# Reading both halves of a product in one VectorE operation: a one-core encoder layer of Strassen-like products

## What is computed

```python
xn = rms_norm(x, attn_norm)
z = xn @ w_in                                   # q | k | v | lru_x | lru_gate | merge gates
attn_branch = windowed_attention(q, k, v) @ w_attn_out
lru_branch  = (rg_lru(conv(xl)) * gelu(yg)) @ w_lru_out
g_a, g_b = split(sigmoid(gl), 2)
x = x + (g_a * attn_branch + g_b * lru_branch) @ w_o
gate, up = split(rms_norm(x, ffn_norm) @ w_gate_up, 2)
x = x + (silu(gate) * up) @ w_down
```

## Time and profile before

| | us |
|---|---|
| median of 3 runs | 1644.11 |
| the profiled execution | 1644.76 |
| its span, first to last instruction | 1643.0 |
| TensorE matmul busy | 1607.5 (98%) |
| VectorE busy | 1027.6 (63%) |
| ScalarE busy | 644.0 (39%) |
| GpSimd busy | 997.6 (61%) |
| granted TensorE clock, mean | 0.993 of full |

### The profile page before, as it was taken

The page is one execution under the profiler, slowest core; times in us unless marked ns, Lnnn a source line. Parts: engine busy times, 40 slices in busy tenths (PEclk is TensorE's granted clock), DMA queues, the critical chain, the costliest instruction groups (busy, mean ns, idle before and its releaser), DMA issues. The chain is left out here.

```text
span 1643.0 us, 28698 instructions
## 1 busy us (share of the span) xinstructions
PE 1607.5 (98%) x11338; PEld 1540.7 (94%) x11338; DVE 1027.6 (63%) x1717; ACT 644.0 (39%) x1322; POOL 997.6 (61%) x714
## 2 busy tenths in 40 slices
PE   7999999999999999999999999999999999999998
PEld 4999999989999898899899989999999999998998
DVE  7677556865646556768798895333333335868695
ACT  5535552354444535424334443333333334333231
POOL 4645543434425251497868529777777778786876
PEclk9999999999999999999999999999999999999999
DMA  5111123213122131373443312222242222373634
GB/s 193 39 52 65 64 72 99 80 66 114 66 97 66 53 114 49 130 291 123 165 149 132 131 39 103 80 78 79 79 184 79 79 79 79 139 271 130 233 142 152
DMA packets 73033, 182.10 MB, mean 111 GB/s; under 512 B 15092, under 2 KB 26676, under 8 KB 72260
## 3 DMA queue, kind: packets, MB, share of 16 engines
q1 hardware_dynamic: 52228, 160.35, 27.7%
q10 hardware_dynamic: 20672, 19.93, 3.8%
HBM read 131.23 MB, written 49.28 MB: 110 GB/s over the span
## 5 line engine op out<-in xcount | busy, mean ns | idle before, releaser
L642 PE MATMUL bank<-xh,wsh 128*128 128x264 f32 x2170 | 620.1, 286 | 8.4 <-DVE spare L1862 3.8
L642 PE MATMUL bank<-xh,wsl 128*128 128x264 f32 x2170 | 616.8, 284 | 0.0
L642 PE MATMUL bank<-xl,wsh 128*128 128x264 f32 x2170 | 616.0, 284 | 0.0
L642 PEld LDWEIGHTS bank<-xh,wsh 128*128 128x128 f32 x2170 | 408.3, 188 | 11.3 <-issue 8.0
L642 PEld LDWEIGHTS bank<-xl,wsh 128*128 128x128 f32 x2170 | 408.4, 188 | 0.2
L642 PEld LDWEIGHTS bank<-xh,wsl 128*128 128x128 f32 x2170 | 408.4, 188 | 0.0
L642 PE MATMUL bank<-acth,wh 128*128 128x352 f32 x960 | 319.3, 333 | 5.6 <-POOL wl L546 4.1
L642 PE MATMUL bank<-acth,wl 128*128 128x352 f32 x960 | 314.7, 328 | 0.0
L642 PE MATMUL bank<-actl,wh 128*128 128x352 f32 x960 | 314.3, 327 | 0.0
L618 POOL TENSOR_TENSOR wsl<-praw,wsh 128x512 fp32r<-128x512 f32 (+1 forms) x157 | 247.6, 1577 | 70.6 <-ACT wsh L1284 70.4
L544 POOL TENSOR_SCALAR wh<-wraw 128x512 fp32r<-128x512 f32 (+1 forms) x100 | 70.9, 709 | 311.9 <-PE bank L642 292.9
(11 more groups left out here) (187 smaller groups left out, 2428.1 us busy)
## 6 DMA issues: line engine op xcount, KB each, us to landing
praw<-in_weights SPq DMA_DIRECT2D x34, 1024.0 KB, 5.0
wraw<-in_weights SPq DMA_DIRECT2D x52, 512.0 KB, 3.3
h_scratch<-ev SPq DMA_DIRECT2D x44, 264.0 KB, 2.1
acc<-h_scratch SPq DMA_DIRECT2D x4, 2112.0 KB, 12.6
ev<-x_scratch SPq DMA_DIRECT2D x6, 1056.0 KB, 5.0
spare<-x_scratch SPq DMA_DIRECT2D x6, 1056.0 KB, 4.9
praw<-in_weights SPq DMA_DIRECT2D x8, 768.0 KB, 5.3
ta_scratch<-tg ACTq DMA_DIRECT2D x24, 176.0 KB, 1.9
```

The costliest lines, as they stand in the source:

```text
L642: return nc.tensor.matmul(*args, **kw)
```

## The change

PSUM is declared as four pairs of banks, so that one access pattern (128 partitions x 2 x 264) covers both halves of a product. In `first_sums` and after products 3 to 6 VectorE does one operation of 528 columns in place of two of 264; it waits for the end of both halves and then counts its semaphore up by 2, so TensorE finds both banks free at once. ScalarE's operations keep their two halves.

Three smaller edits go with it. copy_back is called behind the weights rounded after product 1 instead of those rounded after product 0. In the head, TensorE's `sumsq(1)` goes behind the third raw block; ScalarE gets a small Sqrt between the squares of block 0 and 1, and its rounding of block 0 is cut in two around `root(1)`; VectorE adds block 1's squares in three steps around `rstd(0)`, and `chunk_sum(2)` moves ahead of the second half of `norm(0)` and `rstd(1)`. `combine_hidden` changes as `combine_gated` does and is left out of the diff.

```diff
@@ -390,7 +390,8 @@
             t2raw = tensor(raw, "t2raw", [P, KQ, HALF])
         xl.append(tensor(ctx, "xl6", [P, KQ, HALF], f32r))
 
-        bank = [ctx.enter_context(nc.psum_tensor(f"bank{i}", [P, 512], f32)) for i in range(8)]
+        banks = [ctx.enter_context(nc.psum_tensor(f"banks{i}", [P, 2, 512], f32)) for i in range(4)]
+        bank = [banks[i // 2][:, i % 2, :] for i in range(8)]
@@ -700,8 +701,8 @@
                     raw_block(0, 0)
                     sumsq(0)
                     raw_block(0, 1)
+                    raw_block(0, 2)
                     sumsq(1)
-                    raw_block(0, 2)
                     raw_block(1, 0)
                     sumsq(2)
                     raw_block(1, 1)
@@ -1007,12 +1008,14 @@
                 f(wg[:, 0, c * P:(c + 1) * P], wraw[:, 0, c * P:(c + 1) * P], ACT.Identity, scale=vt[:, c, V_G1:V_G1 + 1])\
                     .then_inc(wg01_done[0], 1)
             squares(0)
+            f(qstd[:, 0, 0:KC], ones[:, 0:KC], ACT.Sqrt)
             squares(1)
             root(0)
             squares(2)
             rstd_row(0)
+            high(0, range(0, 4))
             root(1)
-            high(0, range(KC))
+            high(0, range(4, KC))
             rstd_row(1)
             high(1, range(0, 4))
             root(2)
@@ -1399,7 +1402,7 @@
                             w_high(*made)
                     for made in x_after.get((p, r), ()):
                         x_high(*made)
-                    if r == 0 and p - 1 in (X_FIRST[ATTN_OUT], X_FIRST[OUT]):
+                    if r == 1 and p - 1 in (X_FIRST[ATTN_OUT], X_FIRST[OUT]):
                         copy_back(p - 1)
                     if p == PLAIN - 1 and r == 3:
                         scale_weights()
@@ -1483,12 +1486,18 @@
             for c in range(KC):
                 V.tensor_scalar(wg[:, 1, c * P:(c + 1) * P], wraw[:, 1, c * P:(c + 1) * P], vt[:, c, V_G1:V_G1 + 1], None, ALU.mult)\
                     .then_inc(wg01_done[1], 1)
-            chunk_sum(1, 0, KC, 2)
+            q = xsq[:, 1, :, :]
+            dve.wait_ge(xsq_done, 3)
+            vec(V.tensor_tensor(q[:, 0:2, :], q[:, 0:2, :], q[:, 2:4, :], ALU.add))
             rstd(0)
+            dve.wait_ge(xsq_done, 4)
+            vec(V.tensor_tensor(q[:, 4:6, :], q[:, 4:6, :], q[:, 6:8, :], ALU.add))
+            vec(V.tensor_tensor(q[:, 0:2, :], q[:, 0:2, :], q[:, 4:6, :], ALU.add))
+            V.tensor_tensor(xsum[:, 2, :], q[:, 0, :], q[:, 1, :], ALU.add).then_inc(xchunk_done, 1)
             norm(0, range(0, 4))
+            chunk_sum(2, 0, KC, 3)
+            norm(0, range(4, KC))
             rstd(1)
-            norm(0, range(4, KC))
-            chunk_sum(2, 0, KC, 3)
             norm(1, range(0, 4))
             rstd(2)
             norm(1, range(4, KC))
@@ -1780,18 +1789,24 @@
                 low_done(t, LOWS[t][-1])
                 dve.wait_ge(mm_done, ended(X_FIRST[t], PRODUCTS - 1))
+            def both(r):
+
+                return banks[BANKS[r][0] // 2][:, :, 0:QB]
+
+            def split(a):
+                return a.rearrange("p (n t) -> p n t", t=QB)
+
             def first_sums(p, scale, nres):
 
                 par = (p - PLAIN) % 2 if phase_of(p) == GATE_UP else 0
-                for n in range(2):
-                    q = 2 * nth(p) + n
-                    dve.wait_ge(mm_done, ended(p, 2, n))
-                    dve.wait_ge(s1_done, q + 1)
-                    stt(u2(par, n), bank[BANKS[2][n]][:, 0:QB], scale, u2(par, n), ALU.mult, ALU.add).then_inc(u2_done, 1)
-                    dve.wait_ge(u2_done, q + 1)
-                    if nres:
-                        dve.wait_ge(v_done, 3 * nres)
-                    stt(u4(par, n), bank[BANKS[1][n]][:, 0:QB], scale, u2(par, n), ALU.mult, ALU.add).then_inc(u4_done, 1)
+                q = 2 * nth(p) + 2
+                dve.wait_ge(mm_done, ended(p, 2))
+                dve.wait_ge(s1_done, q)
+                stt(u2(par), both(2), scale, u2(par), ALU.mult, ALU.add).then_inc(u2_done, 2)
+                dve.wait_ge(u2_done, q)
+                if nres:
+                    dve.wait_ge(v_done, 3 * nres)
+                stt(u4(par), both(1), scale, u2(par), ALU.mult, ALU.add).then_inc(u4_done, 2)
@@ -1808,18 +1823,16 @@
                 a = res[b][:, m, :]
                 if r == 4:
                     row_in(p, b)
-                for n in range(2):
-                    dve.wait_ge(mm_done, ended(p, r, n))
-                    if r == 3:
-                        dve.wait_ge(u4_done, 2 * nth(p) + n + 1)
-                    ps = bank[BANKS[r][n]][:, 0:QB]
-                    if r == 4:
-                        stt(a[:, piece(h, n)], a[:, piece(h, n)], 1.0, ps, ALU.add, ALU.mult).then_inc(done, 1)
-                    else:
-                        dst, u = ((u4(0, n), u4(0, n)), None, (u4(0, n), u2(0, n)), (u2(0, n), u2(0, n)))[r - 3]
-                        if r == 5:
-                            dve.wait_ge((merged, gated_done)[t], 3 * p + 1 if t == LRU_OUT else 3 * (p - PAIRS[0]) + 1)
-                        V.tensor_tensor(dst, ps, u, ALU.add).then_inc(done, 1)
+                dve.wait_ge(mm_done, ended(p, r))
+                if r == 3:
+                    dve.wait_ge(u4_done, 2 * nth(p) + 2)
+                if r == 4:
+                    stt(split(a[:, toks(h)]), split(a[:, toks(h)]), 1.0, both(r), ALU.add, ALU.mult).then_inc(done, 2)
+                else:
+                    dst, u = ((u4(0), u4(0)), None, (u4(0), u2(0)), (u2(0), u2(0)))[r - 3]
+                    if r == 5:
+                        dve.wait_ge((merged, gated_done)[t], 3 * p + 1 if t == LRU_OUT else 3 * (p - PAIRS[0]) + 1)
+                    V.tensor_tensor(dst, both(r), u, ALU.add).then_inc(done, 2)
                 dve.wait_ge(done, 2 * nth(p) + 2)
                 half = a[:, toks(h)]
                 if r != 4:
@@ -1851,15 +1864,14 @@
                     return
                 m, h = ((1, 1), (0, 0), (0, 1), (1, 0))[r - 3]
                 done = (c22_done, c11_done, c12_done, c21_done)[r - 3]
-                for n in range(2):
-                    dve.wait_ge(mm_done, ended(p, r, n))
-                    if r != 4:
-                        dve.wait_ge(v_done, 3 * i + {3: 1, 5: 2, 6: 3}[r])
-                    a = res[b][:, m, piece(h, n)]
-                    if p == X_FIRST[OUT] + 1 and r == 3:
-                        x_unused(t)
-                    dst = acc[:, 2 * i + m, piece(h, n)] if t == OUT and p != X_FIRST[OUT] else a
-                    stt(dst, bank[BANKS[r][n]][:, 0:QB], scale, a, ALU.mult, ALU.add).then_inc(done, 1)
+                dve.wait_ge(mm_done, ended(p, r))
+                if r != 4:
+                    dve.wait_ge(v_done, 3 * i + {3: 1, 5: 2, 6: 3}[r])
+                a = res[b][:, m, toks(h)]
+                if p == X_FIRST[OUT] + 1 and r == 3:
+                    x_unused(t)
+                dst = acc[:, 2 * i + m, toks(h)] if t == OUT and p != X_FIRST[OUT] else a
+                stt(split(dst), both(r), scale, split(a), ALU.mult, ALU.add).then_inc(done, 2)
...
```

More of the change, by code:

```diff
@@ L1876, in combine_hidden @@
                 if r != 4:
-                    for n in range(2):
-                        dve.wait_ge(mm_done, ended(p, r, n))
-                        if r == 3:
-                            dve.wait_ge(u4_done, 2 * nth(p) + n + 1)
-                        if r == 5:
-                            dve.wait_ge(h1_done, fp)
-                        dst = (u4(par, n), None, gate(1, n), u2(par, n))[r - 3]
-                        V.tensor_tensor(dst, bank[BANKS[r][n]][:, 0:QB], (u4(par, n), None, u2(par, n), u2(par, n))[r - 3],
-                                        ALU.add).then_inc(done, 1)
+                    dve.wait_ge(mm_done, ended(p, r))
+                    if r == 3:
+                        dve.wait_ge(u4_done, 2 * nth(p) + 2)
+                    if r == 5:
+                        dve.wait_ge(h1_done, fp)
+                    dst = (u4(par), None, gate(1), u2(par))[r - 3]
+                    V.tensor_tensor(dst, both(r), (u4(par), None, u2(par), u2(par))[r - 3], ALU.add).then_inc(done, 2)
                 if r == 6:
```

## The result

The changed kernel takes 1657.13 us (median of 9 runs, 1648.49 to 1662.38) against 1644.11 of the kernel before (9 runs beside it, 1640.82 to 1645.88): a ratio of 1.0072, 95% interval 1.0059 to 1.0086. The forecast was 1648.3, with a range from 1643.4 to 1651.0, so the sign was right and the time was not.

A forecast was written before the change was run, and what follows sets the result against it. TensorE, busy 1607.5 of 1643.0 us, was taken as the bound, so only its gaps counted. Terms of +5.0 (merged reads), 0 (copy_back) and -0.8 (head) gave +4.2 on the 1644.11 median: 1648.3, range 1643.4 to 1651.0.

The forecast's parts named there:

- What bounds the kernel; price of a merged operation: TensorE's gaps bound the kernel; a merged VectorE operation of 528 columns lasts 0.70 us, bounds 0.60 to 0.86.
- The additions 0.55 later and a turn lost: Down projection: VectorE's additions start 0.55 us later, lose a lock turn to GpSimd; waits grow 1.6, 1.6 and 1.25.
- Pair 37, +0.3: Down projection, wait at 1485.28: VectorE was already late, the bank's release comes 0.27 later, so +0.3 us.
- Gate phase and copy_back, 0: The 2.14 us wait at 798.70 goes, but TensorE waits 2.1 longer at 805.15: 0, bounds -1.2 to +0.9.
- The head, -0.8: The 2.34 us wait at 33.88 goes, but GpSimd's low parts limit the gain to 0.8; bounds 0 to 2.3.
- The merged reads: Per pair of operations VectorE gains only 0.07 us, while the first bank is free 0.27 us later.
- What that does after product 2: Down projection: additions start 0.55 us later, lose a lock turn (1.35), plus 0.27 later release: wait grows by 1.6.
- more lost turns: Upper bound for the down projection and tail: up to 1.5 us more if products that only just don't wait lose turns.
- the slow read over two banks: Rival, 0.06: 528 columns take 0.86 us or more and other products begin to wait; 1651.
- the chain that wins a turn: Rival, 0.10: VectorE's shorter chain wins a lock turn (1.72), down-projection waits of 2.2 together go; about 1639.8.
- Late, but no turn lost: Rival, 0.27: GpSimd's turns shift along, down projection and tail cost 3.0, sum +2.2; 1646.3, within 0.2%.
- The rule against grouping: Skill rule: grouping helps a saturated engine, otherwise breaking up can free waiting engines sooner; VectorE stood at 63%.

The follow-up runs named there:

- e3_halves_down: The changed kernel with reads in halves again in the down projection's pairs, except each phase's first (9 of 46 pairs): 1648.66 us, 1.0027.
- e6_delay: The kernel before, nothing merged, with two idle VectorE operations ahead of the additions in the second pair of each down-projection phase: 1649.78 us, 1.0043.
- e12_copy_back_only: The kernel before with copy_back one product later and nothing else changed: ratio 1.0007 (0.9999 to 1.0015).
- e2_edits_only: The kernel before with the edits of the head and of copy_back, without merged reads: 1646.41 us, 1.0021.
- e8_combine_merged: The changed kernel with, in nine down-projection pairs, only the sums after products 3 to 6 merged and the two operations after product 2 in halves: 1649.31 us, 1.0043.
- e11_merges_reordered: The kernel before with all merged reads and VectorE's order altered in the down projection, without head and copy_back edits: 1642.05 us, 0.9980.
- e5_before_reordered: The kernel before, nothing merged, with VectorE's order altered in the down projection so late-wanted additions follow the sum after product 3: 1640.44 us, 0.9976.

## Why the prediction was wrong, step by step

- **What bounds the kernel; price of a merged operation**: right. 0.70 forecast, 691 to 708 ns measured; nothing changes in gate/up.
- **The additions 0.55 later and a turn lost**: right in kind and size, at pairs 35 and 39 (+1.59 and +1.58 where 1.6 was said) and at 43 (+0.99 to +1.08 where 1.25 was, though that turn goes in `e3_halves_down` without a merge too). The additions start 1.61 us after the start of the first merged sum where 1.56 was worked out. GpSimd's operations go first, as worked out, and `e6_delay` gives nearly the same loss from lateness alone. In the changed kernel:

```profile
1436.39 0.71 DVE L1809 SCALAR_TENSOR_TENSOR ev<-banks,ev 128x528 f32<-128x528 f32 x1
1437.20 5.09 DVE L1863 TENSOR_TENSOR spare<-spare,ev 128x528 f32<-128x528 f32 x3
1442.21 3.44 DVE L1697 TENSOR_TENSOR xl<-acc,xh 128x2112 fp32r<-128x2112 f32 x1
```

  The three additions take 5.09 where they took 4.43.
- **Pair 37, +0.3**: 0.62, all from the sums after products 3 to 6.
- **Gate phase and copy_back, 0**: right, within what `e12_copy_back_only` can tell; 2.72 us where about 2.5 was said. That it was so near has luck in it: the same place shows 3.94 and 3.96, with the lower clock, in `e2_edits_only` and `e12_copy_back_only`.
- **The head, -0.8**: wrong, it brought nothing. What I had put down as the bound (chunk_sum(1) held up by the weight split) is what happened. The two run side by side, and the split that should have ended near 23.6 ends at 24.8:

```profile
20.98 1.84 DVE L1495 TENSOR_TENSOR xsq<-xsq 128x704 f32<-128x704 f32 x1
...
25.56 3.16 DVE L1453 TENSOR_TENSOR xsq<-xsq 128x1408 f32<-128x1408 f32 x2
```

```profile
23.38 1.42 POOL L547 TENSOR_TENSOR wl<-wraw,wh 128x512 fp32r<-128x512 f32 x1
24.77 5.91 POOL L552 TENSOR_TENSOR actl<-x,acth 128x352 fp32r<-128x352 f32 x4
30.99 3.60 POOL L552 TENSOR_TENSOR actl<-x,acth 128x352 fp32r<-128x352 f32 x4 [0.31 <-ACT acth L999]
...
38.44 14.39 POOL L552 TENSOR_TENSOR actl<-x,acth 128x352 fp32r<-128x352 f32 x16
```

  The 5.91 and the 3.60 came as worked out, but from 24.77 on and not from 24.1, and with 0.31 of a wait for ScalarE between them. So GpSimd's run of low parts ends where it ended before, at 52.8, and TensorE, which no longer waits at 33.88, waits for 0.96 at 43.20 and for 1.82 in place of 1.01 at 52.89, where it is 0.04 late. Behind that its clock falls:

```profile
54.00:58.00 4.00, 4.00 (x17) 4.00 (x16) 4.00 (x7) 0.00 (x0) 0.00 (x0) 0.57 0.00 0
```

  The lower clock costs about 1.5 us: TensorE is 1.58 late behind it. Up to the second part this comes down to the +1.00 at pair 0. Of the six traces with the head's edits three have this stretch (it isn't in `e2_edits_only`), so the edits themselves brought about nothing, and the 1.00 is the price of a wait near 1.8 us in one execution.
- **The step that failed** is in "The merged reads" and "What that does after product 2", and in the sum of both: each wait was priced at its own length. I let the waits grow from 0.6 to about 2.2 us, and took a microsecond of TensorE for a microsecond. Measured in gate/up, a wait of 1.67 us costs 1.7 and one of 2.06 costs 3.6 in four cases of five; over all traces about every second wait of 1.8 to 2.7 us has the lower clock behind it, for 1.5 us on top. The gap between the +4.2 forecast and the +12.2 of the profiled run, 8.0 us, is made of three such stretches in the down projection (1.52, 1.15 and 1.49, together 4.2), of the head (-0.8 forecast, +1.0 measured, most of it one more such stretch), and of small terms not foreseen: 0.7 between pairs 0 and 33 (0.5 of it the wait at 938.31, 1.95 us where it was 1.43), 0.33 at pair 34, 0.3 at pair 37, 0.35 in pairs 40 to 42 and 0.5 behind pair 43, less 0.2 at pair 43. The upper bound of the range had a term for more lost turns and none for the clock; that is why it was too low. Without the four stretches, 4.2 and about 1.5, the profiled run would be 6.5 later than before, and the bounds of the terms held 7.4 (5.0, 1.5 and 0.9). Two small slips change nothing: 7.4 gives 1651.5 and not 1651, and the lower end, 1643.4, was worked out as 1643.6.
- **The rivals**: the slow read over two banks and the chain that wins a turn are ruled out by 0.70 us and by the four waits. "Late, but no turn lost" held nowhere in the changed kernel, yet how near it was is seen in the runs: the turn at pair 39 is lost in `e2_edits_only` too, which merges nothing, and the one at pair 43 in `e3_halves_down`.
- **The rule against grouping** (the Trainium skill, Perfetto Trace Analysis, Optimizing Scalar/DVE Operations), that breaking work up can free waiting engines sooner, is borne out where bank 6 was wanted at once, by the waits of `e8_combine_merged` at pairs 35 and 37. Where it wasn't, the times don't tell the two forms apart: `e11_merges_reordered` against `e5_before_reordered`.

Not settled: the origin of 0.34 us at pair 37; why the merges lengthen the wait at pair 12; what decides whether a wait near 2 us brings the lower clock; and the head's edits alone, which were not run by themselves. The difference between 1.0021 and 1.0007 would be theirs, but the two intervals overlap, and the trace with 1.0021 also has the lost turn at pair 39.

## What to carry to other kernels

Before merging two short reads of a result, ask who waits for the first of them: the merge saved about 0.07 us of VectorE's time and delayed a release by 0.27, and where the lateness crossed a turn at a shared lock it became 1.6. Price a wait of TensorE by what the clock does behind it: in this kernel's second part its own length up to 1.76 us, 1.5 us on top in half of the cases from 1.78 to 2.72, and in every case from 3.08 on. And look for the operations that stand in front of a release without being wanted yet: the new order was worth 0.24%, where the merges alone cost 0.43%, and with it the merges could no longer be told in the time.

## What was not expected of the hardware

- A single wait of about 2 us in a stretch where TensorE is otherwise without a gap can be followed by 3.41 us at 1.2 GHz, and the same length brings it in one place and not in another (21 of 42 waits of 1.78 to 2.72 us). The busy time doesn't show it; the granted clock does, and so does the count of matmuls, 13 in 2.6 us in place of 21.
- Turns between VectorE and GpSimd are decided by hundredths of a microsecond (0.05 at 1600.00), and losing one costs 1.2 to 1.3 us beside GpSimd's operations of 512 columns and about 0.8 beside those of 384. So a shift far away can change a wait that no edit touched.
